# Hybrid decoder layer: the output projection's convolution half moved ahead of its state-space half

## The reference, cut to what matters

```python
glu = proj[..., :C_CONF] * jax.nn.sigmoid(proj[..., C_CONF:o1])
cconv, new_cbuf = causal_dwconv(glu, cbuf, conf_dw_w, conf_dw_b)
a_out = jax.nn.silu(layernorm(cconv, conf_ln_g, conf_ln_b))
...
y, new_sh = ssd_scan(xs, dt, a_neg, bm, cm, sh.astype(jnp.float32))
y = (y + d_skip * xs) * jax.nn.silu(z)
m_out = rmsnorm(y, groups=4, ssm_norm_g)
out = jnp.concatenate([a_out, m_out], axis=-1) @ w_out
```

## Time and profile before

| | us |
|---|---|
| median of 3 runs | 586.15 |
| lowest and highest | 583.11, 587.26 |
| the profiled execution | 586.09 |
| its span (first to last instruction) | 584.4 |
| PE busy in the span | 540.7 (93%) |
| DVE, ACT, POOL busy | 265.1, 164.1, 85.2 |
| HBM traffic over the span | 280 GB/s |

### The profile page before, as it was taken

The page is one execution under the profiler, slowest core; times in us unless marked ns, Lnnn a source line. Parts: engine busy times, 40 slices in busy tenths (PEclk is TensorE's granted clock), DMA queues, the critical chain, the costliest instruction groups (busy, mean ns, idle before and its releaser), DMA issues.

```text
span 584.4 us, 7620 instructions
## 1 busy us (share of the span) xinstructions
PE 540.7 (93%) x2749; PEld 351.1 (60%) x2749; DVE 265.1 (45%) x783; ACT 164.1 (28%) x386; POOL 85.2 (15%) x103
## 2 busy tenths in 40 slices
PE   5999999997896878999989899999999999999994
PEld 3788888885555657888764334343434343444882
DVE  0799798438447776102253032323232322323653
ACT  3211311116568783502242111111101010102433
POOL 4000063413425540030000000000000000000000
PEclk9999999999989879999989999999999999999997
DMA  8844443687956867793296996999999999999001
GB/s 339 270 145 146 144 145 144 169 238 234 253 181 202 296 232 315 296 370 152 93 384 259 421 422 270 382 423 422 421 423 421 421 422 420 423 419 422 33 0 74
DMA packets 35692, 164.27 MB, mean 281 GB/s; under 512 B 5768, under 2 KB 12744, under 8 KB 19664
## 3 DMA queue, kind: packets, MB, share of 16 engines
q1 hardware_dynamic: 25200, 140.27, 62.1%
q0 software_dynamic: 5920, 21.27, 10.3%
q10 hardware_dynamic: 4544, 2.37, 1.5%
HBM read 155.06 MB, written 8.84 MB: 280 GB/s over the span
## 4 chain that ended last, share of the span: by engine, by line
PE 86%; DVE 7%; issue 2%; DMA 2%; ACT 1%; POOL 1%; DVEq 0%; POOLq 0%; ACTq 0%
PE ps L968 21%; PE ps L1220 19%; PE ps L1067 10%; PE ps L1250 10%; PE ps L1195 5%; PE ps L1283 5%; PE ps L917 2%; DMA asg<-acs_rows 2%; PE ps L1122 2%; DVE xraw_s L1502 1%; PE ps L1153 1%; PE ps L935 1%; PE ps L1147 1%; PE ps L1160 1%; PE ps L959 1%
## 5 line engine op out<-in xcount | busy, mean ns | idle before, releaser
L968 PE MATMUL ps<-u,ring 128*128 128x264 f32 x640 | 145.6, 389 | 0.0
L968 PEld LDWEIGHTS ps<-u,ring 128*128 128x128 f32 x640 | 122.6, 192 | 22.0 <-issue 0.8
L1220 PE MATMUL ps<-ring,xraw 128*64 128x512 f32 x464 | 103.0, 595 | 5.0 <-DVE glu L1714 4.9
L1220 PEld LDWEIGHTS ps<-ring,xraw 128*64 128x64 f32 x464 | 33.9, 137 | 62.6 <-issue 61.1
L1250 PE MATMUL ps<-ring,xraw 128*64 128x512 f32 x256 | 58.5, 598 | 0.7 <-ACT xraw L880 0.7
L1067 PE MATMUL ps<-cat,ring 128*128 128x264 f32 x256 | 57.6, 387 | 1.6 <-DVE cat L1552 1.6
L1067 PEld LDWEIGHTS ps<-cat,ring 128*128 128x128 f32 x256 | 48.5, 190 | 10.6 <-issue 2.4
L632 POOL DMA_INDIRECT xbc<-u_rows,slot_tok x8 | 7.6, 952 | 258.0 <-DVE slot_tok L1669 258.0
L1250 PEld LDWEIGHTS ps<-ring,xraw 128*64 128x64 f32 x256 | 16.9, 136 | 32.1 <-issue 28.8
L558 POOL TENSOR_TENSOR glu<-asg 128x256 f32<-128x256 f32 x8 | 21.4, 2673 | 96.3 <-ACT asg L704 96.3
L1714 DVE COPY glu<-ps 128x264 f32<-128x264 f32 x8 | 3.5, 433 | 68.2 <-PE ps L1260 68.2
(11 more groups left out here) (299 smaller groups left out, 631.8 us busy)
## 6 DMA issues: line engine op xcount, KB each, us to landing
ring<-in_w_moe SPq DMA_DIRECT2D x90, 1024.0 KB, 14.4
ring<-in_w_in SPq DMA_DIRECT2D x20, 1024.0 KB, 5.2
ring<-in_w_out SPq DMA_DIRECT2D x8, 1024.0 KB, 6.1
ring<-in_state_s POOLq DMA_DIRECT2D x8, 512.0 KB, 9.7
out_h_s_out<-ring POOLq DMA_DIRECT2D x8, 512.0 KB, 5.7
ring<-in_w_pleg SPq DMA_DIRECT2D x4, 1024.0 KB, 23.2
asg<-acs_rows ACTq DMA_DIRECT2D x8, 256.0 KB, 6.4
glu<-bc_rows POOLq DMA_DIRECT2D x4, 512.0 KB, 6.4
```

The source lines that it names most:

```text
L968: ins = mm(ps[:, BANK[n], 0:T], wv[:, k, q * P:(q + 1) * P], u[:, k, :], start=(k == 0), stop=(k == KD - 1))
L1220: ins = mm(ps[e * CAP:(e + 1) * CAP, gu, :], xg[:, 4 * hf + k, e * CAP:(e + 1) * CAP], wk, start=(hf == 0 and k == 0), stop=(hf == 1 and k ...
```

## The change

1. The order of the halves is turned round: `w_out_half(n, 0)` is now the convolution half, and SP loads its four weight tiles first. Each half is a closed accumulation. The outputs of the first half rotate through banks 0, 1, 2 and 7 (`AB`), and DVE adds each to `h` on its own (`add_a`), 8 adds that did not exist.
2. The layer norm moves between the items: on PE its mean stands behind item 3 and its variance behind item 5; on DVE the subtraction stands in item 4 and the four multiplies in item 6; on ACT the square stands in item 4 (into `ln_sqr`), the root (Ln, Exp) in item 6 and the eight Silu in item 7.
3. ACT's `decode` stands at items 1, 3, 5 and 7 (states 0 to 3) in place of every item, and states 4 to 7 come behind the last item. DVE's `decode` stands at items 3, 5 and 7 (states 0 to 2) and the other five behind the items, between `gate_y` and `add_a`.
4. The first group mean stands behind the fourth output of the first half, the other three behind the seventh.
5. In SP's queue the first four expert tiles stand behind the fifth tile of `w_out` (n = 24) in place of the third (n = 22), so three tiles of the second half, n = 25, 26 and 27, now stand behind them. Expert tiles 1 to 4 also wait for `ln_stat`. `pool.wait_ge(ln_n, 4)` ahead of the router's weights is gone.

```diff
+        AB = [0, 1, 2, 7]
...
-                    sp.wait_ge(out_used, n - NWIN + 1)
+                    sp.wait_ge(a_psum, 2 * (n - NWIN) + 2)
...
                 else:
+                    sp.wait_ge(ln_stat, 2)
                     sp.wait_ge(out_h_s, 16 * KD)
                     sp.wait_ge(y_s_ready, KD)
...
-                src = w_in[n] if n < NWIN else w_out[n - NWIN]
+                src = w_in[n] if n < NWIN else w_out[(n - NWIN + NWOUT // 2) % NWOUT]
...
-                for j in {22: (0, 1, 2, 3), 23: (4, 5), 24: (6, 7), 25: (8,)}.get(n, ()):
+                for j in {24: (0, 1, 2, 3), 25: (4, 5), 26: (6, 7), 27: (8,)}.get(n, ()):
                     load_first(j)
...
-            pool.wait_ge(ln_n, 4)
...
+                if i == NG:
+                    act.wait_ge(ln_xc, 1)
+                    a.activation(ln_sqr, cat[:, 0:8, :], ACT.Square).then_inc(ln_sq, 1)
                 if i == 6:
+                    act.wait_ge(ln_stat, 2)
+                    link(a.activation(ps[:, 7, 0:T], ps[:, 7, 0:T], ACT.Ln, bias=eps[:, 0:1]))
+                    a.activation(ps[:, 7, 0:T], ps[:, 7, 0:T], ACT.Exp, scale=-0.5).then_inc(g_root, 1)
...
-                decode(i)
+                if i == 7:
+                    for j in range(KD):
+                        act.wait_ge(ln_n, j // 2 + 1)
+                        a.activation(cat[:, j, :], cat[:, j, :], ACT.Silu, scale=par("ln_g", j), bias=par("ln_b", j))\
+                            .then_inc(a_out_ready, 1)
+                if i % 2:
+                    decode(i // 2)
                 for n in AFTER_ITEM[i]:
                     evacuate(n)
...
+            decode(4)
+            decode(5)
+            square_y(0)
+            decode(6)
+            decode(7)
+            for gr in range(1, NG):
+                square_y(gr)
...
+                if i == 3:
+                    pe.wait_ge(conv_done, KD - len(PE_CONV))
+                    pe.wait_ge(conv_s_done, 1)
+                    pe.wait_ge(proj_evac, POS["c", 7, 0] + 1)
+                    pe.wait_ge(btok_ready, 1)
+                    mean_of(cat, 7, mean_k).then_inc(ln_stat, 1)
+                if i == 5:
+                    pe.wait_ge(ln_sq, 1)
+                    mean_of(ln_sqr, 7, mean_k).then_inc(ln_stat, 1)
...
+            pe.wait_ge(proj_evac, NSEQ)
+            pe.wait_ge(xtok_ready, 4)
             for n in range(KD):
-                if n == KD - 1:
-                    pe.wait_ge(ln_n, 4)
-                w_out_half(n, 0)
-                if n == 2:
-                    pe.wait_ge(ln_sq, 1)
-                    mean_of(glu, 7, mean_k).then_inc(ln_stat, 1)
+                if n >= 4:
+                    pe.wait_ge(a_added, n - 3)
+                w_out_half(n, 0).then_inc(a_psum, 1)
+                if n == 3:
+                    pe.wait_ge(y_ready, 2 * NG)
+                    pe.wait_ge(st_ready, 2 * NG)
+                    pe.wait_ge(btok_ready, 2)
+                    group_mean(0)
+                if n == 6:
+                    for gr in range(1, NG):
+                        group_mean(gr)
...
-                if i >= 2:
-                    decode(i - 2)
+                if i == 6:
+                    dve.wait_ge(g_root, 1)
+                    for j in range(0, KD, 2):
+                        v.tensor_tensor(cat[:, j:j + 2, :], cat[:, j:j + 2, :],
+                                        ps[:, 7, 0:T].unsqueeze(1).to_broadcast([P, 2, T]), ALU.mult).then_inc(ln_n, 1)
+                if i in (3, 5, 7):
+                    decode((i - 3) // 2)
...
-            for gr in range(3):
-                gate_y(gr)
-            decode(6)
-            decode(7)
-            gate_y(3)
+            gate_y(0)
+            decode(3)
+            gate_y(1)
+            add_a(0)
+            decode(4)
+            add_a(1)
+            decode(5)
+            gate_y(2)
+            add_a(2)
+            decode(6)
+            add_a(3)
+            decode(7)
+            gate_y(3)
+            for n in range(4, 7):
+                add_a(n)
```

60 lines of the change are left out of this document (22 added, 38 removed).

## The result

| | before | after |
|---|---|---|
| median, us | 585.80 (4 runs) | 594.08 (4 runs) |
| lowest to highest | 583.11 to 587.26 | 593.67 to 595.08 |
| ratio, 95% interval | | 1.016, 1.012 to 1.020 |
| span of the profiled execution | 584.4 | 591.9 |
| mean granted clock | 0.980 | 0.969 |

The changed kernel is 1.6% slower by the ratio in the table (1.4% by the quotient of the two medians). The forecast was 585.4, no change that can be measured, with a range of 579 to 592, so the measured 594.08 lies outside of it. In the profiles the last output of the projection ends at 287.45 before and at 295.11 after (287.72 + 7.39), 7.7 us later, and the spans differ by 7.5. So the whole loss is made by the end of this stage; the expert stage kept its length in this pair of profiles, as predicted.

The account below looks back on a forecast made before the run. PE was taken as the bound (86% of the chain). Of 11.9 us less work, 3.3 went to the later start, 2.7 to the last state and 5.3 to weight tiles, leaving 0.6 to 0.7: 585.4 us, range 579 to 592.

Parts of the forecast that it names:

- step 3: Second half's w_out tiles behind expert tiles in SP's queue: PE waits 5.3 us in all, sixth tile landing at 261.3.
- the term for the lower clock: PE's second half after its waits for tiles: lower clock costs 0 to 1.7 us, taken as 0.
- the wait for the seventh tile: Second half, ahead of outputs 4 and 5: PE stands 3.5 us, with embedding tables moved in the same time.
- Step 1: Items 3 to 7 up to the last evacuation on ACT: first half starts at 217.2, 3.3 us given away.
- rival D: Table switches on ACT cost more than the load, 1.28 us twice each: 5.1 us more, 590.5 us; chance 0.03.
- Step 2: States 4 to 7 decoded behind the items: last group mean at 248.8, PE stands 2.7 us.
- The reload turn: States 5 to 7, from the end of ACT's decode(k) to decode(k+2): 7.9 us, of which 5.1 is landing.
- the case above 8.4 us: State reloads behind the items landing later than about 8.4 us, which costs more than 1% of the run.
- rival C: Lower clock on the path in the second half, behind the wait for tile seven: +3.4 us, 588.8 us; chance 0.06.
- B: Reload turn decides at decode(5) and decode(7) on ACT: at 9.7 us landing everything comes 9.2 later, 594.6 us; chance 0.11.
- Rival A: PE not held by weight tiles in the second half: 580.2 us, or 577.5 without the last state's wait; chance 0.18.
- 11.9 us less of work: Stage to the last output: 61.6 us of work from 217.2, where the stretch from 213.93 took 73.5.

Follow-up runs that it names:

- e1: The changed kernel with all nine early expert tiles behind the last w_out tile in SP's queue; 584.43 us, ratio 0.992 to 1.000.
- e12: The changed kernel with four expert tiles left ahead of the sixth w_out tile and the other five moved behind the last one; 594.23 us.
- e5: The changed kernel with all nine early expert tiles behind the last w_out tile and one load of a table holding Ln and Exp; 578.33 us.
- e6: The changed kernel with each state reload waiting only for the store of its own slot; 593.06 us.
- e10: The changed kernel with each state reload issued one step earlier (slot of state i-1 in place of i-2); 587.77 us.
- e4: The changed kernel without the reloads of states 4 to 7, so that part of the output is not the reference's; 584.83 us.
- e7: The changed kernel with POOL's three embedding tables issued only after the fifth output of the second half; 588.93 us.
- e9: The kernel before, with its nine early expert tiles behind the last w_out tile; 586.20 us, ratio 0.996 to 1.002.
- e3: The changed kernel with one load of a table holding Ln and Exp ahead of item 6's exponential; 590.97 us.
- e11: The changed kernel with w_out tiles ahead of the expert tiles, one Ln and Exp table load, and reloads one step earlier; 574.18 us, ratio 0.979.

## Why the prediction was wrong

**The sum.** It put the end of the last output at 286.7, from a start at 217.2: a stage of 69.5 us. Measured: 80.9, from 214.23 to 295.11. So the end is 8.4 us later than forecast, although the first half started 3.0 us earlier.

**The step that failed** is step 3, the landing of the sixth `w_out` tile. The mechanism was forecast, the size was not: 261.3 forecast, 270.0 measured, 8.7 us. Behind it the term for the lower clock, put at 0, cost 2.6, and the wait for the seventh tile, put at 3.5, did not come: 8.7 + 2.6 - 3.5 = 7.8 of the 8.4. The rest is in hand-overs and in outputs counted at 3.57.

**Step 1, the start: right in its parts.** Items 4 to 7 were predicted at 184.0, 190.1, 199.0 and 209.1 and came at 181.74, 187.44, 196.24 and 206.38: the intervals are within 0.4 us of the forecast, and an offset of 2.0 is there at item 3 already (173.40, where 175.4 was forecast). In e1 and e12, with the same code up to there, the first half started at 216.32 and 216.53, so most of the 3.0 belongs to this one profile. Three loads of 1.28 us stand on ACT at 198.70, 200.46 and 202.15, each with its ACTIVATE 0.01 to 0.02 us behind the end, so rival D fell. By the Trainium skill, "ScalarE: Activation LUTs", section "What ACT_TABLE_LOAD costs", a switch is about 2.66 us with its drain. Neither this profile nor e5, where two loads fewer gave PE 2.7 us (4.81 - 2.10), shows a drain.

**Step 2, the states: the mechanism was right, its terms were too small.** The reload turn was put at 7.9 us with a landing of 5.1. The landings in the profile after are 5.0, 7.5 and 5.4, and I had missed that POOL issues a reload only when the *previous* state's store has landed (`out_h_s >= 16 * i`), which made it stand 4.07 us ahead of the last one. From the start of the first half, `decode(7)` ended 28.8 us on, where 24.7 were forecast. e6 shows that the missed wait is worth only 1.1 of these 4.1, since the reloads then took longer to land (8.0 and 7.9). What does help is to issue each reload one step earlier: in e10 ACT does not wait at all, with landings of 4.8 to 7.2. I had the bound of 9.7 for a landing and gave the case above 8.4 us 0.11; the landings themselves never reached it. PE stood 5.8 us in place of 2.7. On the end of the last output this acts through the store of state 7 alone: it landed at 248.9, 0.9 later than forecast.

**The clock: a term put at zero.** The prediction let the lower clock fall into standing time and took 0 out of "0 to 1.7"; rival C had 3.4 us and a chance of 0.06. Against rows at full clock (means 1.94 and 1.16 and three outputs 10.84 in e10 and e4, four outputs 14.51) the lower clock took 2.1 us on the means (3.03 + 2.13), 1.9 on the next three outputs and 2.6 on the four behind the tile, 6.5 in all. But the prediction's reasoning held for the first two: they lie ahead of the wait for the tile, which is shorter by as much. In e12 the three outputs ran at full clock, and with the wait they took 19.01 us against 19.08. Only the 2.6 behind the tile moved the end.

**Step 3, the transfers: right in kind, wrong by 8.7 us.** The prediction said that the gain is given back here, that the four expert tiles behind the store of state 7 hold the sixth tile of `w_out`, and that PE stands for it. The store took 3.0 (3.3 forecast), SP issued the second expert tile at 248.96 (248.0), and five tiles at 2.46 us would have put the landing at 261.3. It came at 270.0. e7 gives 1.8 to 3.3 of the missing 8.7 to the embedding tables, which I had charged to the seventh tile, reasoning that they were issued later: in another queue that does not help. For the tiles behind, e12 shows nothing beyond the scatter. The rest, 5.4 to 6.9, is not measured by an edit. The stretches show a slow start, 258, 384 and 340 GB/s at 248 to 260 in place of 426, which is (168 + 42 + 86) x 4 = 1.2 MB not moved, 2.8 us, and POOL's other two transfers there, 0.5 MB of the scan's end state and the router's weights, are worth some 1.4 us. These 4.2 are only worked out, why the start is slow is not shown, and 1.2 to 2.7 stay open. In exchange the wait forecast for the seventh tile (3.5) did not come, since this tile was through by the time that PE was that late.

**The rivals.** The time that came is that of B (594.6 forecast, 594.08 measured), but this is chance: by B the last state comes 9.2 us later, and `decode(7)` ended 1.2 later (243.1 against 241.9). Rival A was argued from queues that are empty before 246 in the trace of before. That reading was wrong: at 244 to 248 the DMA share is 0.70 there, with 244 GB/s. The tile order was worth more than the 5.3 of waits that the forecast gave it: e1, which undoes it, shortens the stage by 9.0 and the run by 9.7.

**Was the idea wrong?** It did not pay as it was made, but it can: with the tile order, the table loads and the reloads put right, the run is 12.5 us faster than before (586.69 - 574.18, taken alongside). What the forecast called 11.9 us less of work is 7.4 of the two layer norm means, which moved to places between the items, and for the rest idle time (1.57) and lower clock (2.9) of the kernel before. None of the three repairs was tried on the kernel before except the tile order (e9, nothing), so how much the early reload or the single table load would give there without the change is open.

## What to carry to other kernels

When a consumer's weight tiles share an in-order queue with prefetches that wait for something late, count from the event that frees the queue the whole backlog of every queue, not of its own, and put the tiles that are needed now ahead of the gate. Issue a reload a step ahead, as soon as its slot is free (e10), and do not count on a removed wait giving its full length back (e6). And when a stand of PE is new, ask whether a stretch at the lower clock behind it ends in another wait, which takes it up, or not: here it cost 2.6 us where none followed, and nothing where one did.

## What was not expected of the hardware

In the profile after, each stand of PE in this stage (3.44, 2.37 and 6.34 us) is followed by a granted clock of 0.50 to 0.64 (244 to 256, 268 to 276). It is not a fixed rule of the stand's length: a stand of 2.54 ahead of the first half left the clock at 1.00 in e3 and was followed by 0.60 (216 to 220) in e11, and behind a stand of 3.10 with the same instructions the slow stretch began some 8 us later in e9 than in rows 2. Behind the gate the first transfers were slow: with four or five tiles of 1 MB issued within 4 us, one stretch of 4 us moves 258 GB/s (248 to 252) or 243 (e12, 252 to 256), at a DMA share of 0.87 to 0.89; in e10, where they were issued at 245.9 to 248.2, the stretch from 248 moves 368. And three table loads in a row cost 1.28 us each, nothing more.
